# A shared weight ring for merge and last stage, a subtraction moved in the scan, and table sets named ahead of the norms

## What is computed

```
# first block: convolution branch with layer norm and silu, then out projection and layer norm
y_a = silu(layer_norm(u, ln_a_g, ln_a_b))
h   = layer_norm(alpha * x + mix, ln1_g, ln1_b)
# second block: modulated rms norm, input projection, two scans, merge, experts
h   = modulate(rmsnorm(x, norm1_w), sh1, sc1)
ob  = hgrn2_branch(...)                       # chunked gated scan, 8 heads, 2 directions
mix = (sigmoid(ga) * (o_a @ w_pa) + sigmoid(gb) * (o_b @ w_pb)) @ w_o
x   = x + g1 * mix
t   = modulate(rmsnorm(x, norm2_w), sh2, sc2)
x   = x + g2 * peer(t, w_query, sub_keys, expert_u, expert_v)   # 16384 experts, top 16 of 8 heads
out = rmsnorm(x, final_norm_w)
```

## Time and profile before

| | us |
|---|---|
| median of 3 runs | 4521.23 (4518.48 to 4521.62) |
| profiled execution, time | 4560.65 |
| profiled execution, span | 4558.9 |
| mean granted clock of TensorE in it | 0.957 |
| start and end of the scan stage's instructions | 2775.4, 3048.1 |
| merge | 3053.3, 3216.8 |
| last stage | 3217.9, end |

### The profile page before, as it was taken

The page is one execution under the profiler, slowest core; times in us unless marked ns, Lnnn a source line. Parts: engine busy times, 40 slices in busy tenths (PEclk is TensorE's granted clock), DMA queues, the critical chain, the costliest instruction groups (busy, mean ns, idle before and its releaser), DMA issues. The chain is left out here.

```text
span 4558.9 us, 59527 instructions
## 1 busy us (share of the span) xinstructions
PE 4167.0 (91%) x22056; PEld 3526.8 (77%) x22056; DVE 3308.2 (73%) x4638; ACT 1966.1 (43%) x2339; POOL 930.2 (20%) x821
## 2 busy tenths in 40 slices
PE   8987999999999789999699996989899998999997
PEld 3445777777777568898588885768798998888886
DVE  6336888888888655523498986864577883599998
ACT  1215677777767521101355445653433332333332
POOL 1010000000000100000000003000177777466654
PEclk9988999999999999989799997989899998999999
DMA  9348999999999755524210105633444444899997
GB/s 361 143 173 326 368 366 366 368 368 368 368 367 366 273 202 187 175 84 144 94 40 25 39 17 203 235 135 126 146 146 137 153 152 138 332 417 417 417 415 300
DMA packets 285455, 1077.84 MB, mean 236 GB/s; under 512 B 44628, under 2 KB 65700, under 8 KB 234372
## 3 DMA queue, kind: packets, MB, share of 16 engines
q1 hardware_dynamic: 216228, 864.25, 51.1%
q0 software_dynamic: 68832, 210.11, 11.8%
q10 hardware_dynamic: 192, 0.79, 0.1%
HBM read 919.40 MB, written 155.60 MB: 236 GB/s over the span
## 5 line engine op out<-in xcount | busy, mean ns | idle before, releaser
L1312 DVE TENSOR_TENSOR moe_low<-moe_raw,moe_high 128x2048 fp32r<-128x2048 f32 x256 | 574.5, 2285 | 56.0 <-ACT moe_high L1213 53.0
L3707 ACT ACTIVATE peer_high<-peer_raw 128x1024 fp32r<-128x1024 f32 x272 | 288.0, 1059 | 475.7 <-DMA peer_raw<-expert_v 396.3
L1213 ACT ACTIVATE moe_high<-moe_raw 128x2048 fp32r<-128x2048 f32 x256 | 478.0, 1906 | 1.2 <-PE moe_up_bank L1120 1.2
L3375 DVE TENSOR_TENSOR peer_low<-peer_raw,peer_high 128x1024 fp32r<-128x1024 f32 x272 | 331.3, 1219 | 164.5 <-ACT peer_high L3707 121.6
L3629 POOL DMA_INDIRECT gate_matrix<-peer_whole_gate,peer_cell x336 | 396.1, 1179 | 123.7 <-issue 96.4
L84 PE MATMUL peer_bank<-kept_t_high,peer_high 128*128 128x384 f32 (+1 forms) x1152 | 401.5, 349 | 19.4 <-DVE peer_low L3375 10.9
L86 PE MATMUL peer_bank<-kept_t_high,peer_low 128*128 128x384 f32 (+1 forms) x1152 | 399.4, 347 | 12.6 <-issue 12.1
L85 PE MATMUL peer_bank<-kept_t_low,peer_high 128*128 128x384 f32 (+1 forms) x1152 | 400.5, 348 | 6.7 <-issue 6.4
L84 PE MATMUL peer_bank<-peer_hidden_high,peer_high 128*128 128x384 f32 x1024 | 353.1, 345 | 44.7 <-DVE peer_hidden_low L3497 42.0
L86 PE MATMUL peer_bank<-peer_hidden_high,peer_low 128*128 128x384 f32 x1024 | 344.7, 337 | 0.0
L85 PE MATMUL peer_bank<-peer_hidden_low,peer_high 128*128 128x384 f32 x1024 | 344.7, 337 | 0.0
(11 more groups left out here) (606 smaller groups left out, 10366.6 us busy)
## 6 DMA issues: line engine op xcount, KB each, us to landing
moe_raw<-w_gate_up SPq DMA_DIRECT2D x256, 1024.0 KB
moe_raw<-w_down SPq DMA_DIRECT2D x128, 1024.0 KB
peer_raw<-expert_u SPq DMA_DIRECT2D x128, 512.0 KB
peer_raw<-expert_v SPq DMA_DIRECT2D x128, 512.0 KB
zin_parts_w<-w_in SPq DMA_DIRECT2D x80, 512.0 KB, 3.7
rows<-mix_zero POOLq DMA_DIRECT2D x12, 2048.0 KB, 18.7
gate_matrix<-gla_zeros POOLq DMA_DIRECT2D x32, 768.0 KB, 34.0
hidden<-peer_gelu SPq DMA_DIRECT2D x128, 192.0 KB
```

Source lines behind the costliest of these rows:

```text
L1213: act.activation(high[:, gu_slot[j]], raw[:, gu_slot[j]], ACT.Copy).then_inc(gu_high, 1)
L1312: v.tensor_tensor(low[:, slot], raw[:, slot], high[:, slot].bitcast(F32), ALU.subtract).then_inc(gu_low, 1)
L3375: v.tensor_tensor(low_part[:, slot], raw[:, slot], high[:, slot].bitcast(F32), ALU.subtract).then_inc(cut_low, 1)
L3707: act.activation(high[:, k % 4], raw[:, k % 4], ACT.Copy).then_inc(cut_high, 1)
```

## The change

In words, part by part:

1. **Table sets.** Preloads are added: in the mixer the Ln and Exp set before the wait of either root, and the Silu set after the first; in the input phase the Sqrt set before its waits and the Ln and Exp set after the last copy; in merge the Ln and Exp set after the last sigmoid; in peer the same before the last squares.
2. **Scan.** `low_x` is made by VectorE (`low_tokens`), two pieces after the first direction's kd, ke, qe of period 0 and two after the second's. GpSimd goes from its constants straight to the zeros and their transfers. The norm weight's load moves behind head 0's tiles and gets a semaphore of its own, which VectorE waits for only in `gated`.
3. **Ring shared.** The ring (`raw`, `high`, `low`) and four semaphores `begun` move to the outer scope. In merge SP loads units 0 to 3 of peer as the slots come free (after low parts 21 to 24); ScalarE cuts units 0 to 2 after the squares 5 to 7, VectorE makes their low parts after x3 tiles 6 and 7. Peer begins with `CUT = 3`: its counts are shifted by three, its first loads are units 4 and on.
4. **Merge's tail.** ScalarE adds the shift only to the last 128 columns, into a new tile `last_t`, and makes the high part with the shift in one step from the scaled tile; VectorE makes the low part as (t + shift) - high in one operation.

```diff
+LOG_EXP, SILU, ROOT = "natural_log_exp_and_others", "silu_and_others", "sqrt_and_others"
...
+            act.preload_act_table_set(LOG_EXP)
             act.wait_ge(var_a, 1)
             root(bank[5][:], rooted_a)
+            act.preload_act_table_set(SILU)
...
+            act.preload_act_table_set(LOG_EXP)
             act.wait_ge(var_1, 1)
             root(bank[3][:], rooted_1)
...
                 if tile == EARLY - 1:
+                    act.preload_act_table_set(ROOT)
                     act.wait_ge(scale_made, 2)
...
+            act.preload_act_table_set(LOG_EXP)
             for c in range(DC):
                 act.wait_ge(evicted, c + 1)
...
-            sp.dma_start(lbl[:], d["lb_logits_2"]).then_inc(small, 16)
-            sp.dma_start(nw[:], d["hg_norm_w_2"]).then_inc(small, 16)
...
+            sp.dma_start(lbl[:], d["lb_logits_2"]).then_inc(small, 16)
             load_f(0)
             load_qi(0)
             load_gate(0)
+            sp.dma_start(nw[:], d["hg_norm_w_2"]).then_inc(nw_loaded, 16)
...
-            for n in range(4):
-                part = slice(2 * n, 2 * n + 2)
-                pool.wait_ge(x_high, n + 1)
-                pool.tensor_tensor(low_x[:, part], raw_x[:, part], high_x[:, part].bitcast(F32), ALU.subtract).then_inc(x_low, 1)
...
-            ve.wait_ge(small, 32)
+            ve.wait_ge(small, 16)
...
+            def low_tokens(n):
+                part = slice(2 * n, 2 * n + 2)
+                ve.wait_ge(x_high, n + 1)
+                ve.tensor_tensor(low_x[:, part], raw_x[:, part], high_x[:, part].bitcast(F32), ALU.subtract).then_inc(x_low, 1)
...
                     decayed(p, 0)
+                if p == 0:
+                    low_tokens(0)
+                    low_tokens(1)
...
                     decayed(p, 1)
+                    if p == 0:
+                        low_tokens(2)
+                        low_tokens(3)
...
+            def low_unit(k):
+                v.wait_ge(unit_high, k + 1)
+                v.tensor_tensor(low_part[:, k], raw[:, k], high[:, k].bitcast(F32), ALU.subtract).then_inc(unit_low, 1)
+
+            def low_t(c):
+                v.wait_ge(t_high, c + 1)
+                v.scalar_tensor_tensor(tl[:, c], t[:, c], mod[:, SH2 + c, 0:1], th[:, c].bitcast(F32), ALU.add, ALU.subtract).then_inc(t_low, 1)
...
+                if n > 5:
+                    low_unit(n - 6)
+            low_unit(2)
...
+            for k in range(SLOTS):
+                sp.wait_ge(w_low, TILES - SLOTS + k + 1)
+                sp.dma_start(raw[:, k], peer_unit(d, k)).then_inc(begun[k], 16)
             sp.wait_ge(taken, TILES)
...
+            def cut_unit(k):
+                act.wait_ge(begun[k], 16)
+                act.wait_ge(products, TILES - SLOTS + k + 1)
+                act.activation(high[:, k], raw[:, k], ACT.Copy).then_inc(unit_high, 1)
...
+            act.preload_act_table_set(LOG_EXP)
             for n in range(DC):
                 cut(DC + n + 4)
...
+                if n > 4:
+                    cut_unit(n - 5)
...
-                act.activation(t[:, c], t[:, c], ACT.Identity, bias=mod[:, SH2 + c, 0:1]).then_inc(t_made, 1)
-                act.wait_ge(t_made, c + 1)
-                act.activation(th[:, c], t[:, c], ACT.Copy).then_inc(t_high, 1)
+                act.activation(last_t[:, c], t[:, c, SEQ - P:SEQ], ACT.Identity, bias=mod[:, SH2 + c, 0:1]).then_inc(t_made, 1)
+                act.activation(th[:, c], t[:, c], ACT.Identity, bias=mod[:, SH2 + c, 0:1]).then_inc(t_high, 1)
...
+        CUT = 3
...
-            for k in range(5):
+            for k in range(CUT, 5):
                 next_low()
...
-            for k in range(3):
-                cut(k)
...
+            act.preload_act_table_set(LOG_EXP)
             for c in range(DC):
                 act.wait_ge(dve, c + 1)
```

74 lines of the change are left out of this document (41 added, 33 removed).

## The result

The changed kernel took 4501.58 us in the median of 9 runs, against 4519.22 us for 9 runs of the kernel before: a ratio of 0.9964, interval 0.9954 to 0.9975, or -17.6 us. I had forecast 4509.9 and a range from 4504.0. The profiled execution of after has a span of 4495.9 us and took 4497.77; that of before lay 39 us over its median, so the two spans must not be subtracted. One execution of the kernel before, of 8678 us, is left out of everything that follows.

The account below looks back on a forecast made before the run. It took TensorE, busy 91% of the span, as the bound, with gains only where it waits. Terms of -12.94 us and +1.6 at the scan's start gave -11.3 us, 4509.9 us as the median; range 4504.0 to 4516.5.

Parts of the forecast that it names:

- First block, -1.28: First norm of the first block: the table load before Exp goes, so TensorE starts 1.28 us earlier.
- input norm, -1.45: Norm ahead of the input projection: square root's table load hidden, 1.28 us, and 0.17 us at the second root.
- Merge's tail, -3.7: End of merge: two table loads leave the path, -2.57 us, and the loop over eight chunks shortens, -1.1 us.
- Start of the last stage, -5.13: First units already loaded and cut, TensorE waits only for GpSimd's constants after the barrier: -5.13 us, same slow clock start.
- Rival (c): Last stage's start gains nothing, because something hidden after the barrier holds TensorE: -6.2 us in all, 4515.0; chance 0.08.
- Last norm, -1.38: Last norm: the load before Exp leaves the path and 0.1 us of the load before Ln: -1.38 us.
- Start of the scan, +1.6: Scan's first merged product: earlier zero transfers delay the second weight tile, so TensorE starts 1.6 us later, not 3.0 earlier.
- the share of 0.19: Start of the scan: SP's queue moves 0.19 MB/us while GpSimd's zero transfers run beside it.
- Rival (a): Start of the scan: zero transfers don't slow the tokens, -3.0 us there, -15.9 in all, 4505.3; chance 0.24.
- the sign that I gave for it: Start of the scan: TensorE's first merged product earlier than before would show that the zeros don't slow the tokens.
- "Mostly TensorE's own" chain: Work behind each edited place is a chain, mostly TensorE's, tied to no clock, so a shift passes through whole.
- The rule of a drain: Skill's rule of about 1.38 us drain per table switch: 6.9 us more for five loads; left out of the sum.

Follow-up runs that it names:

- the changed kernel's second run: The changed kernel with no edit, run again for a second profiled execution, measured against the kernel before: ratio 0.9953.
- experiment 4: The changed kernel with GpSimd's zero transfers held back until ScalarE has the scan's second weight tile, run twice: ratios 0.9947 and 0.9961 to the kernel before.
- experiment 3: The scan's part added alone to the kernel before: ratio 0.9987; the changed kernel with only that part undone: 0.9971, both to the kernel before.
- experiment 1: The kernel before with no edit, run three times more: ratios 0.9994, 1.0006 and 1.0000.

## Why the prediction missed, point by point

- **First block, -1.28, and input norm, -1.45**: right as far as the rows go (TensorE's wait for the copied rows 1.28 us shorter; 1.28 less around the square root, and the second load off VectorE's path). The means of the stages, -1.2 and -1.3, agree, but single executions scatter by more than that.
- **Merge's tail, -3.7**: right (-3.7; the loads 2.6 to 2.8, the loop 1.1). VectorE's pitch stayed 0.66 us, so the value taken for the new low part was right, and the cover for the third unit's low part held (VectorE still waits 0.51 us for the root).
- **Start of the last stage, -5.13**: right (-5.2 to -5.3), with GpSimd's constants late next, as said. Rival (c) is refuted. I let the low clock last as long as before, and so it did: 3.0 to 5.9 us from the first product on, 3.7 to 4.4 before, and the U units took 637.3 to 639.0 us, 637.7 to 638.3 before. The 0.65 us that I gave to this in the expectation of the changed kernel's second run is not there.
- **Last norm, -1.38**: the load is gone as forecast.
- **Start of the scan, +1.6**: this step failed, by 2.6 to 2.8 us; it measured -1.0 to -1.2. The chain from the landing of the second weight tile to TensorE was right (13.25 taken, 13.05 found: 2796.27 to 2809.32), and so was the share of 0.19. The mis-sized term was the zeros' start: I let their bytes flow 1.3 us after the issue, and they came some 5 us after it. With 4 us more of the full rate the tile landed 2.4 us sooner. The 1.3 us are right for free engines: in before, issued at 2804.71, the zeros moved 0.70 MB between 2806 and 2808, and held back they began as quickly (issued at 2797.69, 0.20 MB by 2799.6). They are wrong beside a busy queue, and before showed that too, with the sides exchanged: SP issued its next load at 2812.73, but from 2812 to 2816 the zeros' queue moved its full 0.35 MB/us and SP's nothing (windows 2812 to 2814 and 2814 to 2816; no row of q1 in either):

```profile
2812.73 0.33 SPq L2648 DMA_DIRECT2D gla_merged_w<-w_in  x1
...
q0 software_dynamic: 172, 0.69, 100.4%
...
q0 software_dynamic: 174, 0.72, 102.3%
```

  I had taken the share from the window from 2820, where both already flow. What holds the second queue back for these 5 us isn't shown. Rival (a), no slowing at all, is refuted as well, though by the sign that I gave for it (the product earlier than before) it would hold. That sign was too coarse: with a late start of the zeros the product comes earlier and is slowed all the same. ScalarE waits 1.69 us for the first weight tile by DMA in after, and experiment 4 shows 2.1 us of slowing.
- **The sum**: with the scan's start at its measured size it is -13.9 to -14.1, and with the 1.3 us that the expert phase loses -12.6 to -12.8, a term that I had at nothing. The measured gain is 17.7, between 15.2 and 20.2. Some 5 us remain, and only part of them has a name. This is more than the failed step itself, which is under half of the 6 us that the forecast lacked. The rest of the scan was 3.2 us shorter in after's four executions, but they drew 4 dips of the clock against 7, which accounts for 2.0 us (0.75 a run at 2.7); by the counts in experiment 3 dips don't follow the kernel. The wait at the turn and the V units drew about 2.5 us in favour of after beyond the last norm's 1.38, with scatters that took 572.5 to 578.2 us in after and 576.3 to 580.4 in before. These may be draws; no path that I know ties them to the change. One rival isn't ruled out: that the earlier zeros of the scan's part shorten something later. It would fit the 4.4 us of experiment 3; the chain of scatters gives it a little (from the first start to the last end 576 to 582 us in the five undisturbed executions with the zeros as in before, 572 to 579 in the eleven full ones with the zeros early or held back), but the ranges overlap. This remainder stays open.
- **The range** ended at 4504.0, because its lower end was rival (a) with 1 us for scatter. The median of three runs from which I started was 2 us above that of 9, and single executions scatter with a deviation of 4 to 8 us: 1 us was too little.
- **"Mostly TensorE's own" chain** was wrong for the last stage. GpSimd's scatters, 384 at 1.2 and 0.3 us, run from 63 us after the first product to the turn, and TensorE waits for them there. The view behind the earlier trace rows held a warning that I passed over: beside the row shown it had three on "issue", 11.1, 7.6 and 5.3 us, the gaps of experiment 1, so that execution was no picture of this stage. The shift passed through whole all the same, because the first scatter moves with the first queries' products (62.8 to 64.2 us behind them in every execution).
- **The rule of a drain** at each table switch, from the Trainium skill (ScalarE: Activation LUTs, What ACT_TABLE_LOAD costs): the run without preloads speaks against it. The loads there have 0.02 us around them, and the total is -9.9, 4.7 either way, where the rule gives -4.

## What to carry to other kernels

Before a stage is called one engine's, look at a second profiled execution: a stall in the first may have hidden the wait that bounds the others. When work that starts transfers moves ahead, ask when their bytes flow and not when they are issued, and what may be pushed behind: here one wait (zeros only after the last urgent load) starts the scan another 1.5 to 2.1 us sooner. Against before that version came to -20.9 us; it beats the changed kernel in that stage, though its total is not told from the changed kernel's. For a term under the scatter of single runs, read the stage from several profiles, not the total, and read the stages that no edit touches as well: here one of them lost 1.3 us.

## What the runs showed of the hardware

- A queue that started beside a busy one moved its first bytes some 5 us after the issue (GpSimd's at 2777.5 in after, beside SP's at 84.5% of the engines; SP's at 2812.7 in before, beside GpSimd's at 100%); on free engines GpSimd's took 1.3 us.
- A gap of TensorE of 1.3 to 1.4 us may or may not be followed by some 7 us at the low level of its clock; in 18 executions the scan, with the same gap in every period, drew none to three such dips, 2.7 us each.
- GpSimd's indirect transfers, 336 of a kind, took 1.18 to 1.21 us in the mean from one execution to the next, and the chain of 384 scatters was 571 to 581 us long from its first start to its last in the executions without stalls. That moves the end of the kernel by some us.
- One profiled execution in 18 had gaps with no releaser: 27 us of TensorE in the U units, and 42 of VectorE and 51 of ScalarE, at a mean granted clock of 0.97. Its U units took 59 us longer and its last stage 42.
- Seven table loads named ahead went with an expert phase 1.3 us longer, in which none of them stands: 892.3 to 892.7 us against 890.9 to 891.5 over three quarters of its products.
